# Prompt attention with scores transposed: keys on partitions, mask and maximum added in PSUM, row sums split over GpSimd and VectorE

## The reference

```python
def sink_attention(q, k, v, bias, mask, sink):
    s = jnp.einsum('...qhgd,...khd->...hgqk', q, k).astype(jnp.float32) * (HEAD_DIM ** -0.5)
    s = s + bias
    s = jnp.where(mask, s, -jnp.inf)
    m = jnp.maximum(jnp.max(s, axis=-1, keepdims=True), sk)
    p = jnp.exp(s - m)
    w = p / (jnp.sum(p, axis=-1, keepdims=True) + jnp.exp(sk - m))
    return jnp.einsum('...hgqk,...khd->...qhgd', w.astype(v.dtype), v)
```

## Time and profile before

| what | us |
|---|---|
| median of 3 runs | 5122.94 |
| lowest and highest | 5121.25 and 5126.05 |
| the profiled execution: first to last instruction | 5121.8 |
| stage one, to the last store (0 to 2482) | 2482 |
| stage two (2482 to 4523) | 2041 |
| stage three (4523 to the end) | 599 |

### The profile page before, as it was taken

One profiled execution on the slowest core, in us unless ns is written; L12 is line 12 of the kernel. 1 busy time (PEld: TensorE's weight loads), 2 busy tenths in 40 slices (PEclk: granted clock), 3 DMA queues, 4 the chain that ended last, 5 costly groups with the idle time before them and its releaser, 6 DMA issues. The chain is left out here.

```text
span 5121.8 us, 78325 instructions
## 1 busy us (share of the span) xinstructions
PE 4351.6 (85%) x26505; PEld 2716.9 (53%) x26505; DVE 3484.2 (68%) x6644; ACT 3455.7 (67%) x6887; POOL 1618.2 (32%) x1358
## 2 busy tenths in 40 slices
PE   6767778777677877777689999989999999989999
PEld 3334434443333433434366777767777777754444
DVE  1266778888797988989477777787776778625111
ACT  1578788888697787974378888868788885520100
POOL 1345556666647866677310000000000000000000
PEclk9888889888788888988799999999999999999999
DMA  6211111100011011101421111110110010044422
GB/s 143 61 51 45 38 38 36 35 33 36 22 44 39 33 37 44 42 32 46 152 70 56 51 42 39 40 53 31 34 40 28 28 40 24 12 119 134 118 94 103
DMA packets 201975, 276.98 MB, mean 54 GB/s; under 512 B 50496, under 2 KB 134176, under 8 KB 201056
## 3 DMA queue, kind: packets, MB, share of 16 engines
q1 hardware_dynamic: 198624, 271.81, 16.8%
q10 hardware_dynamic: 2960, 0.17, 0.0%
HBM read 156.73 MB, written 114.16 MB: 53 GB/s over the span
## 5 line engine op out<-in xcount | busy, mean ns | idle before, releaser
L595 PE MATMUL bank<-w,x 128*128 128x512 f32 (+1 forms) x2848 | 1256.8, 597 | 23.6 <-DVE w L940 13.5
L1042 DVE TENSOR_SCALAR_CACHE_REDUCE ties<-score,cand 128x512 int8<-128x512 f32 (+13 forms) x448 | 1110.6, 2479 | 123.2 <-POOL score L916 107.9
L595 PEld LDWEIGHTS bank<-w,x 128*128 128x128 f32 x2848 | 575.9, 206 | 612.7 <-issue 547.4
L806 ACT ACTIVATE act_junk<-score,a_cand,a_sign 128x384 int8<-128x384 f32 (+13 forms) x420 | 879.4, 2094 | 14.0
L1833 DVE CUSTOM_DVE_ANT_0 row<-bank,mask 128x512 f32<-128x512 f32 (+3 forms) x1024 | 622.6, 639 | 179.8 <-PE bank L1572 178.5
L613 PE MATMUL bank<-kiT,qi 128*128 128x512 f32 (+3 forms) x1136 | 395.3, 490 | 408.6 <-ACT relu L736 206.4
L1539 POOL TENSOR_TENSOR near_bias<-table,mask 128x2048 f32<-128x2048 f32 (+1 forms) x32 | 129.5, 4048 | 1763.9 <-DVE part L1833 1748.3
L1767 ACT ACTIVATE pT<-bank 128x512 f32<-128x512 f32 (+2 forms) x704 | 368.7, 524 | 426.2 <-PE bank L1588 424.0
L1669 ACT ACTIVATE row<-row,top 128x1024 f32<-128x1024 f32 (+7 forms) x640 | 632.8, 990 | 4.0 <-DVE top L1846 4.0
L1588 PE MATMUL bank<-ident,row 128*128 128x128 f32 x4224 | 593.7, 281 | 26.4 <-DVE pT L1944 19.5
L1572 PE MATMUL bank<-kT,qb 64*128 64x256 f32 (+1 forms) x4352 | 608.4, 396 | 8.7 <-DVE part L1833 5.4
(11 more groups left out here) (255 smaller groups left out, 4882.6 us busy)
## 6 DMA issues: line engine op xcount, KB each, us to landing
qk_t<-ring SPq DMA_DIRECT2D x66, 256.0 KB, 2.0
gates<-ring SPq DMA_DIRECT2D x66, 256.0 KB, 2.0
gate<-gates SPq DMA_DIRECT2D x33, 512.0 KB, 3.4
out<-x_in SPq DMA_DIRECT2D x33, 512.0 KB, 2.9
x<-in_x_prompt SPq DMA_DIRECT2D x32, 512.0 KB, 3.7
mixed<-mixT SPq DMA_DIRECT2D x64, 256.0 KB, 2.1
mix_in<-mixed SPq DMA_DIRECT2D x32, 512.0 KB, 4.2
x_in<-in_x_prompt SPq DMA_DIRECT2D x32, 512.0 KB, 3.8
```

Source lines behind the costliest of these rows:

```text
L595: ins = pe.matmul(p_bank[n % 2][:, 0:n1 - n0], held[:, c * P:(c + 1) * P], w[:, c, n0:n1], start=(c == 0), stop=(c == KC - 1))
L806: tick(act.activation(junk, row, ACT.Sign, bias=c, scale=back, accum_out=a_sum[:, :]))
L1042: n = tick(dve.tensor_scalar(ties[:, 0:width], row, c.bitcast(F32), 0.0, ALU.is_ge, ALU.add, accum_out=counts[:, i:i + 1]))
```

## The change

Stage two is written anew; stages one and three change a little to fit.

- A unit is one query tile and one key tile of a group, for all 8 heads: 63 of group A and 528 of group B, 591 in all. Scores come with keys on partitions: two f32 matmuls of 512 columns (4 heads of 128 queries), the keys being the stationary side. So what comes out of the exponential can be multiplied by v as it is, and no transposes or copies of them are needed.
- With keys on partitions the mask and the maximum vary along both directions. Both are added in PSUM by four bf16 matmuls of 256 columns a unit: the stationary side is the mask with ones in one half of its rows (`held`), the moving side (`shift`) holds unit matrices and diagonals of minus the maximum. For the 126 units near the diagonal DVE adds the relative bias in PSUM (`add_bias`, 1024 columns) before the exponential.
- ACT exponentiates all 1024 columns of a unit in one instruction, PSUM to SBUF, with no bias and no accumulator.
- Row sums: GpSimd adds the units' first 512 columns into one buffer (`acc[..][:, 0:512]`), DVE the other 512, and once a tile and group 16 records of one-column matmuls sum over the partitions.
- The maximum must be known before the scores are made, so it is found a tile ahead: the old scores, queries on partitions, are made once more (`max_b`, 512 keys and one head of each half a slot; `max_a`), into one auxiliary pair of PSUM banks, and DVE runs the same add-and-maximum over them, writing back into PSUM. A single auxiliary pair also takes the sums, the gate's transposes (8 at once), the swap of the maximum's halves and, at the start, the bias tables. PE waits before each auxiliary use until DVE has done with the one before.
- The mask is loaded twice a tile, once for the maximum, once in two halves for `held`. `chosen` is stored in one piece a tile.
- The output's head order changes, so the gates are written, and `w_out` is loaded, in another order (16 DMAs of 64 rows instead of 8 of 128); in stage three one matmul takes the place of two narrower ones.

The diff, cut to its core:

```diff
-CLASSES = [(2 + 4 * c, min(6 + 4 * c, TILES), c + 1) for c in range(8)]
+UNITS = []
+for _t in range(TILES):
+    UNITS += [(_t, 0, _b) for _b in range(max(_t - 1, 0), _t + 1)] + [(_t, 1, _b) for _b in range(_t + 1)]
+def max_slots(t):
+    return [("max_a", t, j) for j in range(2)] + [("max_b", t, c, g) for c in range(0, (t + 1) * P, STEP) for g in range(GROUP)]
+for _t in range(TILES):
+    AUX[min(OWN_A[_t] + 3, LAST_STEP)].append(("sums", _t, 0))
+    AUX[min(END[_t] + 4, LAST_STEP)].append(("sums", _t, 1))
+    AUX[min(END[_t] + 6, LAST_STEP)].append(("gate", _t))
+for _t in range(1, TILES):
+    _lo, _hi = START[_t - 1] + (1 if _t > 2 else 0), max(END[_t - 1] - 2, START[_t - 1])
+    _slots = max_slots(_t)
+    for _n, _s in enumerate(_slots):
+        LAST_MAX[_t] = _lo + _n * (_hi - _lo + 1) // len(_slots)
+        AUX[LAST_MAX[_t]].append(_s)
+    AUX[min(LAST_MAX[_t] + 1, END[_t - 1])].append(("swap", _t))
...
+            def accumulate(i):       
+                to = acc[a][t % 2][:, 0:STEP]
+                pool.wait_ge(s_exp, i + 1)
...
+                pool.tensor_tensor(to, held_in, pT[i % RING][:, 0:STEP], ALU.add).then_inc(s_acc, 1)
...
+            for i in range(N_UNITS):
+                for t in range(2, TILES):
+                    if i == START[t - 1] + 1:
+                        make_near(t)
+                if i in ACC_AT:
+                    accumulate(i)
...
+            def score(i):
+                if i >= 2:
+                    pe.wait_ge(s_exp, i - 1)
...
+                for vh in range(KVH):
+                    rows = slice(vh * HD, (vh + 1) * HD)
+                    pe.matmul(s[:, vh * STEP:(vh + 1) * STEP], keys[rows, :].bitcast(F32),
+                              q[t % 2][rows, a, :, :].bitcast(F32).rearrange("p g n -> p (g n)"), start=True, stop=False)
+                for c in range(2):
+                    for vh in range(KVH):
+                        ins = pe.matmul(s[:, vh * STEP:(vh + 1) * STEP].rearrange("p (g c n) -> p c g n", g=GROUP, c=2)[:, c],
+                                        masks[:, c, cols], shift[t % 2][:, c, a * HEADS + vh * GROUP:a * HEADS + (vh + 1) * GROUP, :],
+                                        start=False, stop=(c == 1))
...
+            def apply(i):
+                for vh in range(KVH):
+                    rows = slice(vh * HD, (vh + 1) * HD)
+                    ins = pe.matmul(oT[a][rows, :], value[:, rows], pT[i % RING][:, vh * STEP:(vh + 1) * STEP],
+                                    start=(b == first_of(t, a)), stop=(b == t))
...
+            def extra(x):
+                n = AUXN[x]
+                if n:
+                    pe.wait_ge(s_auxd, n)
...
+                elif kind == "max_b":
+                    for vh in range(KVH):
+                        ins = pe.matmul(aux[:, vh * STEP:vh * STEP + w], q[t % 2][rows, 1, g, :], kT[rows, c:c + w], start=True, stop=True)
...
+                elif kind == "sums":
+                    for h in range(HEADS):
+                        ins = pe.matmul(aux[:, h:h + 1], acc[a][t % 2][:, h * P:(h + 1) * P], ones[:, 0:1], start=True, stop=True)
...
+            for i in range(LAST_STEP + 1):
+                if i < N_UNITS:
+                    score(i)
+                for x in AUX[i][0:1]:
+                    extra(x)
+                if 0 <= i - LAG < N_UNITS:
+                    apply(i - LAG)
+                for x in AUX[i][1:]:
+                    extra(x)
...
+                act.activation(pT[i % RING][:, :], slots[i % 2], ACT.Exp).then_inc(s_exp, 1)
...
+            def add_bias(i):
+                dve.tensor_tensor(slots[i % 2], slots[i % 2], bias[:, a, b - t + 1, :], ALU.add).then_inc(s_biased, 1)
+            def accumulate(i):
+                to = acc[a][t % 2][:, STEP:]
...
+                dve.tensor_tensor(to, held_in, pT[i % RING][:, STEP:], ALU.add).then_inc(s_accd, 1)
...
+                            s = aux[:, vh * STEP + c0 - c:vh * STEP + c0 - c + w]
+                            ins = dve.tensor_tensor_reduce(s, s, more,
+                                                           1.0, PAD, ALU.add, ALU.max, part[:, h, at:at + 1])
...
+            for i in range(LAST_STEP + 1):
+                if i in BIASED:
+                    add_bias(i)
+                for x in AUX[i]:
+                    use(x)
+                if i - 1 in ACC_AT:
+                    accumulate(i - 1)
+                for _ in range(LATE_DVE[i]):
+                    next(late_work, None)
```

More of the change, by code:

```diff
@@ L1201, in job_whose_row @@
-def job_whose_row(n):
-    t, k = divmod(n, 6)
-    if k >= 4:
-        return n - 2
-    return n - 4 if t else n - 2
-def spread(items, steps):
-    for i, item in enumerate(items):
-        PLAN[steps[i * len(steps) // len(items)]].append(item)
-def steps_of(*jobs):
-    return [(n, g) for n in jobs for g in range(n_steps(n))]
-PLACED = {(_n, _g): [] for _n in range(N_JOBS) for _g in range(n_steps(_n))}
-for _n in range(N_JOBS):
-    _t, _k = divmod(_n, 6)
-    if _k >= 2:
-        _from = job_whose_row(_n)
-        for _j in range(len(score_units(_n))):
-            PLACED[_from, min(_j, n_steps(_from) - 1)].append(("score", _n, _j))
-    elif _t:
-        PLACED[_n - 2, n_steps(_n - 2) // 2].append(("score", _n, 0))
-    if _k == 2:
-        PLACED[_n, n_steps(_n) - 1].append(("gate", _t, 0))
-    if _k == 0 and _t:
-        PLACED[_n, 0].insert(0, ("gate", _t - 1, 1))
@@ L1233 @@
-UNIT = {("score", 0, 0): 0, ("score", 1, 0): 1}
-TOP_AT = {0: 0, 1: 1}
-for _n in range(N_JOBS):
-    for _g in range(n_steps(_n)):
-        for _u in PLACED[_n, _g]:
-            UNIT[_u] = len(UNIT)
-            if _u[0] == "score" and _u[1] % 6 < 2:
-                TOP_AT[_u[1]] = len(TOP_AT)
-    for _m in range(_n, min(_n + 5, N_JOBS)):
-        if _m % 6 >= 2 and job_whose_row(_m) == _n:
-            TOP_AT[_m] = len(TOP_AT)
-UNIT["gate", TILES - 1, 1] = len(UNIT)
-def units_through(n):
-    return max(at for (kind, m, j), at in UNIT.items() if kind == "score" and m <= n) + 1
@@ new lines, in parts_of, with part_column @@
+def parts_of(t, c):
+    width, far = (t + 1) * P, (t + 1) * P - near_of(t)
+    end = min(c + STEP, width)
+    return [(c0, c1 - c0, near) for c0, c1, near in ((c, min(end, far), False), (max(c, far), end, True)) if c1 > c0]
+def part_column(t, c):
+    return sum(len(parts_of(t, x)) for x in range(0, c, STEP))
+AUX = {_i: [] for _i in range(-1, LAST_STEP + 1)}
+AUX[-1] = [("bias", a, n) for a in range(2) for n in range(2)] + max_slots(0) + [("swap", 0)]
+LAST_MAX = {0: -1}
+for _t in range(TILES):
+    AUX[min(OWN_A[_t] + 3, LAST_STEP)].append(("sums", _t, 0))
+    AUX[min(END[_t] + 4, LAST_STEP)].append(("sums", _t, 1))
+    AUX[min(END[_t] + 6, LAST_STEP)].append(("gate", _t))
@@ L1478, in _ @@
[L1478 to L1489 removed]
+                    sp.wait_ge(s_lstore, 16 * (LATE_TILES.index(t) + 1))
@@ L1490, in load_late, with load_gate @@
+            def load_gate(t):
+                if t:
+                    sp.wait_ge(s_gp, t)
+                sp.dma_start(gate[:, :], gates[t]).then_inc(s_gate, 16)
             def load_late(i):
@@ new lines, in _ @@
+            load_q(0)
+            load_keys(0)
+            load_keys(1)
+            sp.wait_ge(s_made, 2)
+            sp.wait_ge(s_eyes, 2)
+            load_mask(0)
+            load_held(0, 0)
+            load_va(0)
+            load_values(0)
+            load_q(1)
+            load_va(1)
+            load_gate(0)
+            load_mask(1)
+            load_values(1)
+            for i in range(2, PARTS):
+                load_keys(i)
+                load_values(i)
+            sp.dma_start(a_k_prompt[0, 0].rearrange("t h d -> t (h d)"), values[TILES - 1, :, 2 * P:3 * P]).then_inc(s_win, 16)
@@ new lines, in exponential_sinks, with copy_output @@
+            def exponential_sinks(t):
+                act.wait_ge(s_top, t + 1)
+                if t >= 2:
+                    act.wait_ge(s_auxd, AUXN["sums", t - 2, 0] + 1)
+                act.activation(sink_e[t % 2][:, :], sink_d[t % 2][:, :], ACT.Exp).then_inc(s_sink, 1)
+            def copy_output(t, a):
+                act.wait_ge(s_pv, UNIT[t, a, t] + 1)
+                if t >= 2:
+                    act.wait_ge(s_auxd, AUXN["gate", t - 2] + 1)
+                act.activation(o_sb[t % 2][:, a * STEP:(a + 1) * STEP], oT[a], ACT.Copy).then_inc(s_evac, 1)
@@ new lines, in _ @@
+            dve.wait_ge(s_made, 1)
+            for c in range(2):
+                rows, others = slice(c * HD, (c + 1) * HD), slice((1 - c) * HD, (2 - c) * HD)
+                tick(dve.memset(held_a[rows, c, :], 0.0))
+                tick(dve.tensor_copy(eye64[rows, :], ident[rows, rows]))
+                tick(dve.tensor_copy(swap[rows, others], ident[rows, rows]))
+                for i in range(2):
+                    tick(dve.tensor_copy(shift[i][rows, c, :, :], ident[rows, rows].unsqueeze(1).to_broadcast([HD, 2 * HEADS, HD])))
@@ L2129, in _ @@
```

(4 more changed lines are left out.)

889 lines of the change are left out of this document (367 added, 522 removed).

## The result

The changed kernel takes 5506.8 us in the median (5499.6 to 5513.8) against 5124.5 before: slower, ratio 1.0743 with a 95% interval of 1.0728 to 1.0758. The forecast was 5590 in a range of 5320 to 5840. The profiled execution has a span of 5505.9 us, 384 more than before. Stage one is as it was, and stage three takes 599 us, as before, so stage two takes 5505.9 - 599 - 2482 = 2425 us, where it took 2041 (forecast 2510).

What follows compares the result with a forecast made beforehand. PE was taken as the bound: stage two's 2196 us of PE work, 206 of waits, 38 `near_bias`, 60 start and 10 end make 2510 against 2041; +469 less 3 gives 5590 us, range 5320 to 5840.

Steps and rivals of the forecast that it cites:

- `max_b` is the old score work again, in 512-column passes: 0.86: PE's auxiliary work in stage two: 0.86 us for each of 528 tile pairs plus 576 x 0.11, 517 us.
- The clock still 1.00: Sign expected in the changed profile: PE's granted clock stays at 1.00, the 2.4 GHz level.
- the guess that a 512-column pass covers the weights' arrival: PE's scores and products: a 0.43 us pass hides late weights, so fixed cost is 0.10 a phase, 0.96 in all.
- The rival that fixed costs go: Rival for PE's phases: loads hidden at every change of phase, stage two 2219 us, total 5300; chance 0.15.
- the one of passes set by weight loads: Rival for PE: loads, not columns, set passes; a 512-column pair takes 0.215 us, total 4960; chance 0.08.
- The one-item step: Stage-two step with one auxiliary item: PE starts one every 3.4 us and waits for nothing.
- two signs that would make it wrong: In the changed profile: a one-item step under 3.0 us, or PE work under 2000 us.
- The second item waits 0.66: PE at a step's second auxiliary item: waits 1.62 - 0.96 = 0.66 us for DVE, 203 times, 134 us.
- `near_bias`, 1.2 us a tile: GpSimd's 4.11 us operation once a tile blocks DVE's add and delays the bias: 1.2 us a tile, 38 us.
- The accumulator in PSUM, "nothing to 0.1 an item": DVE's add-and-maximum writing its result into PSUM instead of SBUF: nothing to 0.1 us an item.
- The start: Stage two's first scores wait behind tables, their conversion, transposes and first maximum: 20 us more, 60.
- faster had 0.08: Chance given to the kernel getting faster, by the rival that weight loads set PE's passes (total 4960).

Runs made afterwards that it cites:

- two-pass run: Maximum's matmuls (`max_b`, `max_a`) read operands as plain f32 instead of fp32r, against the changed kernel (5507 us): 5815.4 us, +309.

## Why the prediction was right, point by point

It was right in direction and range, and 83 us too high. Of its mechanism one half holds, that PE sets the pace and waits for DVE's round trip at the single auxiliary pair. The other half, that PE's work alone exceeds the old stage, does not, and that the total came so close is in part luck: terms that were 358 us too high stand against others that were some 275 too low. The stage by its terms, in us (measured phases by their median length at full clock, the low clock in a line of its own, as what is left of PE's busy time):

| term | forecast | measured |
|---|---|---|
| scores, 591 x (0.96; 1.06) | 567 | 626 |
| masks, 591 x (0.54; 0.54) | 319 | 319 |
| products, 591 x (0.96; 1.01) | 567 | 597 |
| `max_b` | 517 | 230 |
| `max_a` | 68 | 27 |
| sums, 64 x (1.8; 1.88) | 115 | 120 |
| gates, swaps, tables | 42 | 39 |
| low clock on all of these | 0 | some 120 |
| PE's waits, boundaries included | 244 | 307 |
| start (2482 to 2520), end | 70 | 40 |
| stage two | 2510 | 2425 |

- **"`max_b` is the old score work again, in 512-column passes: 0.86"** is the step that failed. The diff has a bitcast to F32 on the scores and none on the maximum, so it is one pass: 0.43 a phase. The two-pass run shows that this one difference is worth 309 us; with it, the kernel takes 5815, and the forecast would have been 225 too low.
- **"The clock still 1.00"** failed the other way. PE at 87% in bursts is not PE at 97%: 0.92, and some 120 us of longer matmuls (the sum of the phases less their full-clock lengths). The prediction asked what PE waits for, never what the wait costs afterwards.
- **The unit.** Masks at 0.54 were exact; four matmuls take 4322.67 - 4322.13 = 0.54, forecast 4 x 0.11 + 0.10. By the formula of the Trainium skill's "TensorE: Matmul & The Clock Gate", section Back-to-back issue gap, they are 0.109 each, 0.44 in all, an estimate; the phase of 0.54 fits it with 0.10 of fixed cost, and this row can't tell the two apart. Scores kept 0.20 of fixed cost and products 0.15: the guess that a 512-column pass covers the weights' arrival was wrong, +89 us. The rival that fixed costs go is refuted with it, as is the one of passes set by weight loads (two pass pairs would be 0.43 in all, and are 1.01 and 1.06).
- **The one-item step** was forecast at 3.42 ("every 3.4 us") and is 3.04: just the missing pass and the fixed costs. The prediction named two signs that would make it wrong. A one-item step under 3.0 did not come, by 0.04. PE work under 2000 us did: 1958 at full clock, against 2196 forecast (2078 with the low clock in it).
- **"The second item waits 0.66"**: 0.63 in the rows above. But the round trip is a floor for every pair of neighbours (2.13), not only within a step, and so the sum was 307 and not 244. It has 34 us in it of the five long waits beside the late search's close, which the prediction left out; 14 us of such waits were in the old stage too.
- **`near_bias`, 1.2 us a tile**: splitting it gained 19 us of the 38 forecast. That GpSimd blocks DVE there was the right mechanism, but it came at five places and not once a tile.
- **The accumulator in PSUM, "nothing to 0.1 an item"**: the operation lasts 714 ns on average where it had 688, and two of them with the last read of the accumulator take 1.41 (4309.94 to 4311.35) against the forecast's 1.30: 0.1 an item, its upper end.
- **The start**: the first scores come at 2533.6, 40 us after the old ones; stage three, forecast 3 us shorter, is not shorter.
- **The side on which the time fell**: faster had 0.08 by a mechanism that isn't there. That PE's work alone, 1958 us at full clock, is slightly less than the old stage's 2041 was not seen; with full-clock matmuls, no waits and the 40 us of start and end the change would have been worth about 40 us, by this sum. It is slower by its waits (307) and its clock (120), not by its work.

## What to carry to other kernels

Trading transposes for a second pass of the scores is no trade in PE time alone: count how many times two engines hand a single buffer back and forth, and set the full round trip (2.13 us here), which neither engine's busy share shows, against the work that lies between every two uses. If the buffer can't be doubled, space its uses evenly in time and not by loop step; that alone gave 78 us. Read each matmul's operand types before pricing it, and after a change that thins out PE, price the clock too.

## What was not expected of the hardware

- Matmuls of one column, ahead of which only 0.41 us was idle, were followed by the lower clock level; taking 7 of 8 away took the stage's granted clock from 0.92 to 0.96 and 59 us beyond their own length.
- Unread matmuls in PE's waits made the program 32 us faster.
- A two-pass phase costs 0.63 more than a one-pass one, although the pass itself is 0.43. That the second pass's weights come late, as in the earlier trace rows, would explain it; it was not tested.
- One phase's place matters: a maximum item directly between scores and masks makes a one-item step 2.84 in place of 3.04 in the median, with the same matmuls. The item's matmuls start 0.56 behind the start of the scores there (4327.37 and 4327.93) and not 1.06, and the masks 1.29 behind it and not 1.49, so scores and item overlap in part. Why the order allows this was not tried.
